# Expert weights of a mixture-of-experts layer: load order by free buffer, and a fifth gate-and-up buffer

## The reference, cut to what matters

```
z = RMSNorm(x)                                  # 544 tokens x 1024
group = top 1 of 4 groups;  experts = top 2 of the group's 4     # 16 experts in all
h  = silu(z @ w_gate[e]) * (z @ w_up[e])        # w_gate, w_up: 1024 x 256 for each expert
x += sum over the 2 chosen e of  comb[e] * (h @ w_down[e])       # w_down: 256 x 1024
y  = RMSNorm(x) * final_norm
```

## Time and profile before

| | |
|---|---|
| runs | 1456.78, 1457.37, 1460.93 us; median 1457.37 us |
| profiled execution | 1453.02 us, of which the trace's span is 1451.3 us |
| PE busy | 1125.6 us, 78% of the span; mean granted clock 0.865 |
| DVE, ACT, POOL busy | 39%, 27%, 14% |
| DMA | 231.97 MB, mean 160 GB/s |
| experts' loop, `gate_up(0)` to the last `down` | 1130.25 to about 1417.3 us of the span |

### The profile page before, as it was taken

One profiled execution on the slowest core, in us unless ns is written; L12 is line 12 of the kernel. 1 busy time (PEld: TensorE's weight loads), 2 busy tenths in 40 slices (PEclk: granted clock), 3 DMA queues, 4 the chain that ended last, 5 costly groups with the idle time before them and its releaser, 6 DMA issues. The chain is left out here.

```text
span 1451.3 us, 25096 instructions
## 1 busy us (share of the span) xinstructions
PE 1125.6 (78%) x8927; PEld 829.4 (57%) x8927; DVE 570.2 (39%) x1607; ACT 387.0 (27%) x863; POOL 203.6 (14%) x329
## 2 busy tenths in 40 slices
PE   6899995386798689898989858978677866666690
PEld 4799994243655477777767626977575322222230
DVE  3733346536377123344443416465256111001115
ACT  1300004411277134333444320125224100000012
POOL 2000000000200525544335000000000110111103
PEclk9999998556599689999999857999898888888895
DMA  6244433500740977769888342304272676777615
GB/s 187 43 88 87 123 102 110 177 1 14 256 155 1 204 177 197 205 179 225 214 209 221 109 133 51 88 28 175 88 280 86 241 293 254 297 287 292 273 54 191
DMA packets 179382, 231.97 MB, mean 160 GB/s; under 512 B 75992, under 2 KB 148680, under 8 KB 169880
## 3 DMA queue, kind: packets, MB, share of 16 engines
q1 hardware_dynamic: 155032, 175.32, 38.9%
q0 software_dynamic: 20128, 53.28, 12.2%
q10 hardware_dynamic: 4128, 2.10, 0.8%
HBM read 239.99 MB, written 30.98 MB: 187 GB/s over the span
## 5 line engine op out<-in xcount | busy, mean ns | idle before, releaser
L2815 PE MATMUL bank<-wgu,memtok 128*64 128x512 f32 x384 | 126.6, 638 | 81.6 <-issue 79.8
L2815 PEld LDWEIGHTS bank<-wgu,memtok 128*64 128x64 f32 x384 | 41.1, 147 | 162.8 <-issue 162.8
L1408 POOL DMA_DIRECT2D rawc<-in_cache_nsa_kv x128 | 75.2, 588 | 152.1 <-PE bank L1839 132.4
L273 PE MATMUL bank<-h_high,w_low 128*128 128x272 f32 x384 | 81.1, 293 | 5.3 <-DVE h_low L389 2.9
L1714 DVE COPY ZTs<-bank 128x512 f32<-128x512 f32 x64 | 44.1, 690 | 100.0 <-PE bank L1767 100.0
L3035 DVE COPY yT<-bank 128x256 f32<-128x256 f32 x16 | 6.8, 424 | 194.6 <-PE bank L2826 194.6
L273 PE MATMUL bank<-h_low,w_high 128*128 128x272 f32 x384 | 80.6, 291 | 0.0
L273 PE MATMUL bank<-h_high,w_high 128*128 128x272 f32 x384 | 79.9, 290 | 0.0
L2815 PE MATMUL bank<-xn_tok,memtok 128*64 128x512 f32 x128 | 68.2, 694 | 0.0
L1408 POOL DMA_DIRECT2D ring<-in_cache_nsa_kv x112 | 65.7, 587 | 14.3 <-issue 7.4
L273 PE MATMUL bank<-n_high,w_low 128*128 128x272 f32 x256 | 56.0, 301 | 14.7 <-DVE n_low L389 8.1
(11 more groups left out here) (580 smaller groups left out, 2287.6 us busy)
## 6 DMA issues: line engine op xcount, KB each, us to landing
kv<-in_cache_nsa_kv SPq DMA_DIRECT2D x256, 128.0 KB, 4.0
wdn<-in_exp_w_down SPq DMA_DIRECT2D x32, 1024.0 KB, 4.9
wgu<-in_exp_w_gate SPq DMA_DIRECT2D x24, 1024.0 KB, 15.2
wgu<-in_exp_w_up SPq DMA_DIRECT2D x24, 1024.0 KB, 17.5
rawc<-in_cache_nsa_kv POOLq DMA_DIRECT2D x128, 128.0 KB, 3.7
ring<-in_cache_nsa_kv POOLq DMA_DIRECT2D x112, 128.0 KB, 5.6
ring<-in_w_in SPq DMA_DIRECT2D x44, 256.0 KB, 3.7
rows_dram<-zrow POOLq DMA_DIRECT2D x16, 512.0 KB, 14.4
```

The source lines that it names most:

```text
L273: mm = pe.matmul(out, a, c[:, at:at + out.shape[1]], start=start and m == 0, stop=stop and m == 2)
L1408: return eng.dma_start(dst[64 * half:64 * half + 64, :, :, :].rearrange("p a c n -> p a (c n)"), cache[bass.ds(page, 1), :, :, kinds, :].r ...
L2815: mm = pe.matmul(gemm_big[n % 2][half, :].rearrange("p (m f) -> p m f", m=2), XT[:, n % 2, k, half], w[j][:, :, k, :], start=(k == 0), sto ...
```

## The change

There is a fifth gate-and-up buffer (`GR` = 5), `fifth`, in the place of the residual in `xT`, so gate and up of load s use buffer s modulo 5, down still s modulo 4. The gain gets a tensor of its own (4 KB in each partition). SP's queue is written in another order: load 3 as before; then gate and up of load 4 as soon as the residual has been turned (`tk_out`), and the gain; then, for n = 1 to 15, wait for `gate_up(n - 1)`, issue gate and up of loads 2n+3 and 2n+4 (for n = 1 loads 5 and 6, for n = 14 load 31, for n = 15 none), wait for `down(n - 2)` (from n = 2), issue down of loads 2n and 2n+1. PE's order, its matmuls, and all that DVE, ACT and POOL do are the same; only the index of the buffer and of its semaphore change on PE.

```diff
-            WR = 4
+            WR, GR = 4, 5
...
-            gain = x_flat[:, 0:D]
+            fifth = x_flat[:, 0:2 * KT * FF].rearrange("p (m n) -> p m n", m=2)
...
-                return fourth if j == WR - 1 else wgu[:, j, :, :]
+                return fifth if j == WR else fourth if j == WR - 1 else wgu[:, j, :, :]
...
+            gain = t11("gain", [P, D])
...
+                def filled(sp, s):
+                    slot = LOADS[s]
+                    if slot < NE:
+                        return slot, None
+                    if not table:
+                        sp.wait_ge(late_ready, 1)
...
+                    return table["expert"][slot - NE], table["used"][slot - NE]
...
-                        if s < WR:
-                            sp.wait_ge(xn_saved, 16 * NQ)
-                        else:
-                            sp.wait_ge(gu_mm, (s - WR) // 2 + 1)
-                        load_gate_up(sp, gate_up_at(s % WR), s % WR, e, cond)
-                        if s >= WR:
-                            sp.wait_ge(y_mm, (s - WR) // 2 + 1)
-                        load_down(sp, s % WR, e, cond)
-                        if s == WR:
-                            sp.wait_ge(tk_out, 4 * NQ)
-                            sp.dma_start(gain[:, :], ...).then_inc(gain_here, 16)
+                    sp.wait_ge(xn_saved, 16 * NQ)
+                    load_gate_up(sp, gate_up_at(WR - 1), WR - 1, *filled(sp, WR - 1))
+                    load_down(sp, WR - 1, *filled(sp, WR - 1))
+                    sp.wait_ge(tk_out, 4 * NQ)
+                    load_gate_up(sp, gate_up_at(WR), WR, *filled(sp, WR))
+                    sp.dma_start(gain[:, :], ...).then_inc(gain_here, 16)
+                    for n in range(1, NPR):
+                        sp.wait_ge(gu_mm, n)
+                        for s in range(GR, NSL):
+                            if (s - GR) // 2 == n - 1:
+                                load_gate_up(sp, gate_up_at(s % GR), s % GR, *filled(sp, s))
+                        if n >= 2:
+                            sp.wait_ge(y_mm, n - 1)
+                            for s in (2 * n, 2 * n + 1):
+                                load_down(sp, s % WR, *filled(sp, s))
...
-                            pe.wait_ge(gu_here[(2 * n + j) % WR], 32 * (2 * n // WR + 1))
+                            pe.wait_ge(gu_here[(2 * n + j) % GR], 32 * ((2 * n + j) // GR + 1))
...
-                        w = [gate_up_at((2 * n + j) % WR).rearrange("p m (k f) -> p m k f", k=KT) for j in range(2)]
+                        w = [gate_up_at((2 * n + j) % GR).rearrange("p m (k f) -> p m k f", k=KT) for j in range(2)]
```

More of the change, by code:

```diff
@@ L2538, in build @@
             cross.close()
-            WR = 4
+            WR, GR = 4, 5
             wgu = ctx.enter_context(nc.sbuf_tensor("wgu", [P, 3, 2, KT * FF], F32, side="right"))
             wdn = ctx.enter_context(nc.sbuf_tensor("wdn", [P, WR, 2 * D], F32, side="right"))
-            gu_here, dn_here = [sem(f"gu_here{j}") for j in range(WR)], [sem(f"dn_here{j}") for j in range(WR)]
+            gu_here, dn_here = [sem(f"gu_here{j}") for j in range(GR)], [sem(f"dn_here{j}") for j in range(WR)]
             gate_w, up_w = (I[n][0].rearrange("e (p k) f -> e p (k f)", p=P) for n in ("exp_w_gate", "exp_w_up"))
@@ L2672, in build @@
             with nc.Block() as block:
+                table = {}
+                def filled(sp, s):
[4 more added lines that the diff above has]
+                        sp.wait_ge(late_ready, 1)
+                        _, table["expert"] = nc.values_load_multi_w_load_instructions(
+                            late_i[0:1, 0, 0:NOV], engines=[mybir.EngineType.SP], min_val=0, max_val=NE - 1)
+                        _, table["used"] = nc.values_load_multi_w_load_instructions(
+                            late_i[0:1, 1, 0:NOV], engines=[mybir.EngineType.SP], min_val=0, max_val=1)
+                    return table["expert"][slot - NE], table["used"][slot - NE]
                 @block.sync
@@ L2678, in _ @@
                         sp.dma_start(xn_dram[P * q:P * q + rows_of[q], :], xn_tok[0:rows_of[q], q, :]).then_inc(xn_saved, 16)
[L2679 to L2690, removed]
-                        if s < WR:
-                            sp.wait_ge(xn_saved, 16 * NQ)
-                        else:
-                            sp.wait_ge(gu_mm, (s - WR) // 2 + 1)
-                        load_gate_up(sp, gate_up_at(s % WR), s % WR, e, cond)
-                        if s >= WR:
-                            sp.wait_ge(y_mm, (s - WR) // 2 + 1)
-                        load_down(sp, s % WR, e, cond)
-                        if s == WR:
-                            sp.wait_ge(tk_out, 4 * NQ)
-                            sp.dma_start(gain[:, :], I["final_norm"].rearrange("(a n) -> a n", a=1).to_broadcast([P, D]))\
-                                .then_inc(gain_here, 16)
@@ new lines, in _ @@
+                    sp.wait_ge(xn_saved, 16 * NQ)
[3 more added lines that the diff above has]
+                    load_gate_up(sp, gate_up_at(WR), WR, *filled(sp, WR))
+                    sp.dma_start(gain[:, :], I["final_norm"].rearrange("(a n) -> a n", a=1).to_broadcast([P, D]))\
+                        .then_inc(gain_here, 16)
+                    for n in range(1, NPR):
[7 more added lines that the diff above has]
+                                load_down(sp, s % WR, *filled(sp, s))
```

## The result

The changed kernel takes 1375.13 us (median of four runs, 1371.27 to 1379.26) against 1457.07 us; the ratio is 0.9436, 95% interval 0.9401 to 0.9470. Timed once more, beside other kernels, it was 0.9457 (0.9433 to 0.9480). So about 79 to 82 us are gone. Forecast were 75.7 us and 1381, range 1375 to 1399: the direction and the place are right, the time is at the lower edge of the range, and two terms of the sum were each wrong by 13 us or more, in opposite directions.

The account below looks back on a forecast made before the run. Late-issued odd loads bound the kernel; afterwards PE's own pace would. Loop loss 76.7 us less 1.0 for DMA gives 75.7; the median 1457.4 - 75.7 = 1381.7, rounded 1381, range 1375 to 1399.

Parts of the forecast that it names:

- two terms of the sum: Loop over pairs 2 to 14: 76.7 us of loss removed, less 1.0 us for the DMA engines.
- What bounded the kernel: Loop: odd pairs' gate and up loads, queued behind the even load's down weights, exposed six waits of 11.2 to 12.3 us.
- A clean pair of 13.02 us: Pair that waits for nothing: 7.09 + 0.44 + 0.90 + 3.58 + 1.01 us; thirteen make 169.3 of 245.91, so 76.7 lost.
- price 1 us: Loop: 410 GB/s asked against 400 taken; 4 us too slow in all, covered by a 6.6 us lead; 1 us charged.
- Rival A: Loop: DMA engines become the bound; 1387 us at 380 GB/s, 1402 at 350; chance 0.20, over 1385.
- nothing gained, nothing lost: Fifth buffer, before pair 1: load 4 leaves at about 1133.2 instead of 1139.14, pair 1 starts at 1141.09 either way.
- B: Down of even pairs: late down weights stop PE 3 to 6 us each, six times; 1399 to 1417 us; chance 0.06.
- C: Row gathers in the loop come late and set the pace; slower, 1524 us at a 30 us gather; chance 0.02.
- D: Odd pairs' gaps: the exposed wait isn't the issue behind down, so the change does nothing; 1457 us; chance 0.02.
- the 17.1 worked out: Down weights in the loop: five loads at 400 GB/s, 13.1 us, plus 4; needed after 22.5, fitting by 5.4.
- The formula of C: Loop: with a gather of L us a pair lasts L + 3 - 8.5, deciding from 24.5 us on.
- Signs: Gate-ups 13.0 us apart, last near 1324, none over 7.2; clock 1.00; DMA near 385 GB/s; SP's down waits shrink.

## Why the prediction was right and where it was wrong

**What bounded the kernel: right.** The odd load behind the even load's down was the cause, and the new order alone removes all six long waits. What was to bound it afterwards, PE's own pace, was wrong from pair 6 on, for the two reasons that follow.

**A clean pair of 13.02 us: wrong, and this is the step that failed.** The prediction counted "1.01 us of a gap for which no releaser is shown" as part of a pair that waits for nothing. It was a wait like the others: the skipped load's issue, held behind a down. Clean is 11.78 us: the gap goes, and gate-up takes 6.87 instead of 7.09 us when it follows without one. The loss in the loop was therefore 245.9 - 153.1 = 92.8 us, not 76.7; with pair 1 and the tail the floor lies 18.0 us deeper than the sum had it. The sign was in the trace: pairs 2, 12 and 15 had 1.50, 1.34 and 0.71 us in place of 1.01, which a gap of PE's own would not do.

**The DMA engines: price 1 us, measured 14.3.** The capacity was estimated well: 400 GB/s was taken, and 416 over 59 us and 395 over the next 95 were measured. The demand was wrong, because it hung on the clean pair: 10.7 MB in 26.04 us is 410 GB/s, in 23.56 us it is 454, over the 380 to 417 of the earlier trace rows and over the 416. From pair 6 on two pairs take 26.5 to 27.0 us (the downs at 1226.35, 1253.30 and 1279.81). At 416 GB/s they would take 25.7. The engines have dips: 330 GB/s from 1248 to 1252 us, with SP's next issue at 1251.83, and 225 from 1292 to 1296, with the next at 1295.28. That they come from PE's stops, which free buffers late so that SP issues late, is argued and not shown. Rival A named the right mechanism, and its sign came (gaps ahead of odd gate-ups from the middle of the loop on, at a DMA share of 1.0), with the wrong time (over 1385); the forecast named the wrong bound with nearly the right time. That was luck: the gain was 18.0 us too small, the loss 13.3 too small, and 75.7 + 18.0 - 13.3 = 80.4, as in the windows.

**The level.** The prediction took its gain off the median of before, 1457.4, and not off the profiled execution, which was 4.3 us lower. For a median that is the right base. By medians 81.9 us are gone (79.0 when timed again) where 75.7 were forecast; 4.7 of the difference are the two terms, and the rest, 1.5 us more or 1.4 less, is smaller than the 8 us between the four runs of the changed kernel. The lower end of the range has a small slip: 0.3% under 1457.4 is 1453.0 and not 1452.5, which still gives 1376.

**The fifth buffer "nothing gained, nothing lost": wrong by 5.2 us** of the loop (172.6 against 167.4). For the early load 4 by itself it holds (0.7 us). The fifth buffer also lets SP issue every even load a pair sooner; that this is where the other 4.5 us come from is argued, since no run has the one without the other.

**Rivals B, C, D.** B: there are waits ahead of down, but three of 0.4 to 0.7 us. The down weights landed 22.8 to 23.2 us after their issue, some 6 us later than the 17.1 worked out, and at the true pace only 11.78 + 6.87 + 1.34 = 20.0 us are allowed and not 22.5; the stops are so short because each comes behind a wait of 1.9 to 2.7 us ahead of the gate-up before. C: no transposes waited for a gather inside the loop; a gather took about 11 us. The formula of C is wrong: from the end of down of pair n to the transposes of pair n+4 it is two pairs less 4.48 us (0.90 + 3.58), so a pair would last (L + 7.5) / 2, which is the old mean of 18.9 at L = 30.3 and not 24.5, and its 1524 falls with it. At the pace of 11.78 a gather decides from 16.1 us on. D: out. The Trainium skill, "DMA: Bandwidth & Descriptors", section Bandwidth, puts a core's HBM side near 358 GB/s, and says that each core gets about that when both cores of an HBM domain (two cores that share a memory) stream. Here one core runs; it had 416 over 59 us, so in this case that limit doesn't apply.

**Signs.** SP's waits and the place of the loads came as said. The gate-ups are 11.8 and not 13.0 us apart, up to pair 6. The last starts at 1323.7 (near 1324 was said), but from a loop that begins 1.7 us later and is 2.8 us shorter than the 170.2 forecast. None was to take over 7.2 us, and one took 8.79; the clock is 0.99 over the loop, not 1.00; the loop's rate is 370 GB/s, not 385.

## What to carry to other kernels

A gap that returns with the same length need not be the engine's own: look at what the other queues issue in the last tenth of a microsecond before it ends, skipped and empty instructions included. A queue that waits for buffers should be written in the order in which they come free; here an additional buffer before that was worth nothing. When a stall goes, work out the demand on the next resource at the new pace, with the bytes spread over the stretch up to the last one that is due: unused slots at the end of a list are free time that comes too late.

## What the runs showed of the hardware

- The DMA engines carried 416 GB/s over 59 us and 411 over 95 us beside matmuls without a pause, at a granted clock of 1.00, and the matmuls were none the slower: 6.87 us for gate-up with the engines full, and 6.87 from 1323.69 on, where they move 43 GB/s. The engines had 417 GB/s over 16 us of the kernel before in which PE was busy for 6.47, so they lost nothing either.
- A skipped conditional DMA took 0.07 to 0.11 us of SP's queue, and who waited for it went on 0.08 us after SP had reached it; with the skipped loads and the waits for them taken out, the gap of 1.01 us was gone.
- Reading the 32 values of the late slots into SP's registers took about 10 us (in the kernel before from 1119.7, when they were written, to the next issue at 1130.48; with experts 3 and 4 first from 1151.6 to 1162.39).
- Whether the clock falls with a short gap isn't told by the gap's length alone: in the kernel with the new order and four buffers the gate-up after a gap of 2.52 us took 8.78 us (mean granted clock 0.81), that after 3.77 us took 7.09 (1.00), and that after 3.79 us took 9.64 (0.73).

```profile
1188.50 2.52 issue
1191.02 8.78 PE bank L2821 x32
...
1241.28 3.77 issue
1245.05 7.09 PE bank L2821 x32
...
1295.62 3.79 issue
1299.41 9.64 PE bank L2821 x32
```
